# Near attention in the feed-forward: probabilities normalised on GpSimd before they are turned, results kept as [d, rows]

## The reference, cut to what matters

```python
logits = einsum('bcqgrd,bckgd->bcgrqk', qc, kb) * (d ** -0.5)   # 8 heads of 64, 2 key heads
logits = where(valid, logits + bias, NEG)
p = softmax(concatenate([logits, sink], axis=-1), axis=-1)[..., :-1]
o = einsum('bcgrqk,bckgd->bcqgrd', p, vb)
```

## Time and profile before

| | us |
|---|---|
| median of 3 runs | 3340.32 |
| lowest, highest | 3338.69, 3345.28 |
| span of the profiled execution | 3341.9 |

### The profile page before, as it was taken

The page is one execution under the profiler, slowest core; times in us unless marked ns, Lnnn a source line. Parts: engine busy times, 40 slices in busy tenths (PEclk is TensorE's granted clock), DMA queues, the critical chain, the costliest instruction groups (busy, mean ns, idle before and its releaser), DMA issues.

```text
span 3341.9 us, 43563 instructions
## 1 busy us (share of the span) xinstructions
PE 3248.2 (97%) x16120; PEld 2720.3 (81%) x16120; DVE 1947.1 (58%) x3598; ACT 1450.4 (43%) x2610; POOL 1704.8 (51%) x1077
## 2 busy tenths in 40 slices
PE   8999999999999999999999999999999999999998
PEld 6788878878777888888788887877888789878887
DVE  3236747558566556567666766867768678621112
ACT  3324435335454444345455534736655367420001
POOL 5555554454345555553555554145556731356665
PEclk9999999999999999999999999999999999999999
DMA  5745454444524333323433332063333410333332
GB/s 159 206 136 167 120 169 133 130 126 150 178 97 140 98 107 97 119 84 121 155 103 106 95 117 92 1 224 97 95 102 107 142 44 1 124 123 95 96 106 95
DMA packets 446562, 388.99 MB, mean 116 GB/s; under 512 B 20976, under 2 KB 376560, under 8 KB 445712
## 3 DMA queue, kind: packets, MB, share of 16 engines
q1 hardware_dynamic: 424912, 341.99, 33.7%
q10 hardware_dynamic: 21440, 44.22, 3.6%
HBM read 323.37 MB, written 62.78 MB: 116 GB/s over the span
## 4 chain that ended last, share of the span: by engine, by line
PE 90%; DVE 3%; ACT 3%; POOL 2%; issue 1%; DMA 1%; ACTq 0%; SPq 0%; DVEq 0%; POOLq 0%
PE BANK L849 21%; PE BANK L851 21%; PE BANK L850 21%; PE LP L849 3%; PE LP L851 3%; PE LP L850 3%; PE BANK L1072 3%; PE LP L1056 2%; PE BANK L1087 2%; PE LP L957 2%; PE LP L956 2%; PE LP L1057 2%; PE BANK L1089 1%; PE BANK L1098 1%; POOL WLO L819 1%
## 5 line engine op out<-in xcount | busy, mean ns | idle before, releaser
L817 POOL TENSOR_SCALAR WHI<-WRAW 128x1024 fp32r<-128x1024 f32 x456 | 507.6, 1113 | 1217.2 <-PE BANK L851 985.4
L819 POOL TENSOR_TENSOR WLO<-WRAW,WHI 128x1024 fp32r<-128x1024 f32 x456 | 1108.0, 2430 | 37.9
L849 PE MATMUL BANK<-H2hi,WHI 128*128 128x512 f32 x1408 | 558.3, 396 | 2.7 <-POOL WLO L819 1.9
L851 PE MATMUL BANK<-H2hi,WLO 128*128 128x512 f32 x1408 | 550.8, 391 | 0.0
L850 PE MATMUL BANK<-H2lo,WHI 128*128 128x512 f32 x1408 | 550.8, 391 | 0.0
L849 PE MATMUL BANK<-HThi,WHI 128*128 128x512 f32 (+1 forms) x1024 | 404.2, 395 | 3.4 <-DVE QS L1706 3.4
L851 PE MATMUL BANK<-HThi,WLO 128*128 128x512 f32 (+1 forms) x1024 | 399.7, 390 | 0.0
L850 PE MATMUL BANK<-HTlo,WHI 128*128 128x512 f32 (+1 forms) x1024 | 399.7, 390 | 0.0
L1443 ACT ACTIVATE MASK<-SCD,THR 128x896 bf16<-128x896 f32 (+5 forms) x186 | 281.8, 1516 | 218.5 <-DVE THR L1766 190.7
L851 PEld LDWEIGHTS BANK<-H2hi,WLO 128*128 128x128 f32 x1408 | 265.5, 189 | 56.8
L849 PEld LDWEIGHTS BANK<-H2hi,WHI 128*128 128x128 f32 x1408 | 266.1, 189 | 54.1 <-issue 2.3
(11 more groups left out here) (291 smaller groups left out, 6514.5 us busy)
## 6 DMA issues: line engine op xcount, KB each, us to landing
WRAW<-in_w_in SPq DMA_DIRECT2D x124, 512.0 KB, 4.5
WRAW<-in_w_ffn_gate SPq DMA_DIRECT2D x88, 512.0 KB, 3.9
WRAW<-in_w_ffn_up SPq DMA_DIRECT2D x88, 512.0 KB, 3.8
WRAW<-in_w_ffn_down SPq DMA_DIRECT2D x88, 512.0 KB, 3.5
qsp<-QS SPq DMA_DIRECT2D x32, 512.0 KB, 5.7
gates<-GS ACTq DMA_DIRECT2D x64, 256.0 KB, 2.2
WRAW<-in_w_out SPq DMA_DIRECT2D x32, 512.0 KB, 4.3
GL<-gates ACTq DMA_DIRECT2D x48, 256.0 KB, 4.1
```

Source lines behind the costliest of these rows:

```text
L817: nc.gpsimd.tensor_scalar(hi, raw, 1.0, 1.0, ALU.mult, ALU.mult).then_inc(w_hi, 1)
L819: nc.gpsimd.tensor_tensor(lo, raw, hi.bitcast(f32), ALU.subtract).then_inc(w_split, 1)
L849: nc.tensor.matmul(dst, whi, mhi, start=first, stop=False)
L851: return nc.tensor.matmul(dst, wlo, mhi, start=False, stop=last)
```

## The change

The sum and its inverse move forward, to two slots ahead of the first turn. GpSimd then multiplies the unit's 128 x 1024 exponentials by the inverse of their row, in place (`near_norm`), in its program behind the split of the job in which the first turn stands; PE's turns wait for that multiply. The turn-back, the scaling and the last transposes are gone. After the second value block ScalarE copies the low half (64 partitions) to `NLV`, and VectorE adds it to the high half out of the bank, with two instructions that write `OTA`. In units with `NEAR_FIRST[q] % 4` other than 1, both turns and the first value block come one slot later; the second value block and the copy come at 13 instead of 12 in all units, the adds at 14. The values bank is free for the next unit when `near_kept` is signalled by VectorE's adds, no longer by ScalarE's copy. ScalarE waits for `near_kept` ahead of the first split of `OTA`.

```diff
         def near_after(q):
-            return (2, 5, 9, 8) if NEAR_FIRST[q] % 4 == 1 else (3, 6, 10, 9)
+            return (2, 5, 9, 8) if NEAR_FIRST[q] % 4 == 1 else (3, 7, 11, 10)
+
+        NEAR_LAST = 13
...
+            def near_norm(b, q):
+                j, hs = q // 2, slice(4 * (q % 2), 4 * (q % 2) + 4)
+                pool.wait_ge(near_inverted, n(near_inverted, (b, q)))
+                nc.gpsimd.tensor_tensor(NLG[q % 2][:, :, :], NLG[q % 2][:, :, :], RS[:, j, hs].unsqueeze(2).to_broadcast([P, 4, BAND]),
+                                        ALU.mult).then_inc(near_normed, made(near_normed, (b, q)))
...
                 if key[0] != "br" or key[2] > 1:
                     split(i)
+                k, place = pair_place(key[1], key)
+                for q in NEAR[k] if k is not None else ():
+                    if place == (NEAR_FIRST[q] + near_after(q)[1]) // 2:
+                        near_norm(key[1] + 1, q)
...
-                            pe.wait_ge(near_probs, n(near_probs, (b, q)))
+                            pe.wait_ge(near_normed, n(near_normed, (b, q)))
...
-                                near.bank = take("near_values", near_copied, (b, q), ("near v", b, q))
+                                near.bank = take("near_values", near_kept, (b, q), ("near v", b, q))
...
-                    if since == 15:
-                        dst = take("near_back", near_scaled, (b, q), ("near x", b, q))
-                        pe.wait_ge(near_copied, n(near_copied, (b, q)))
-                        pe.wait_ge(fold_set, 1)
-                        for i in range(4):
-                            last = nc.tensor.matmul(dst[:, i * HD:(i + 1) * HD], NXV[:, i, :], FOLD[:, :], start=True, stop=True,
-                                                    skip_group_check=True)
-                        last.then_inc(near_back, made(near_back, (b, q)))
-                    if since == 18:
-                        dst = take("near_back", near_kept, (b, q), ("near o", b, q))
-                        for e in range(2):
-                            last = nc.tensor.transpose(dst[:, e * P:(e + 1) * P],
-                                                       NON[:, 2 * e:2 * e + 2, :].rearrange("p h d -> p (h d)"), IDENT[:, :])
-                        last.then_inc(near_out, made(near_out, (b, q)))
...
             def split_head(b, s, e):
+                if b and (s, e) == (0, 0):
+                    act.wait_ge(near_kept, n(near_kept, (b, PAIRS // 2 - 1)))
...
-                    if since == 18:
-                        act.wait_ge(near_out, n(near_out, (b, q)))
-                        nc.scalar.copy(OTA[:, 2 * g:2 * g + 2, j * P:(j + 1) * P],
-                                       in_tiles(bank(("near o", b, q)))[:, 0:2, :]).then_inc(near_kept, made(near_kept, (b, q)))
...
-                    if h - NEAR_FIRST[q] == 12:
+                    if h - NEAR_FIRST[q] == NEAR_LAST:
                         act.wait_ge(near_valued, n(near_valued, (b, 2 * q + 1)))
                         if q:
-                            act.wait_ge(near_out, n(near_out, (b, q - 1)))
-                        nc.scalar.copy(NXV[:, :, :], in_tiles(bank(("near v", b, q)))).then_inc(near_copied, made(near_copied, (b, q)))
+                            act.wait_ge(near_kept, n(near_kept, (b, q - 1)))
+                        nc.scalar.copy(NLV[0:HD, :, :], in_tiles(bank(("near v", b, q)))[HD:P, :, :]
+                                       ).then_inc(near_copied, made(near_copied, (b, q)))
...
-                    if since == 10:
+                    if since == near_after(q)[1] - 2:
                         dve.wait_ge(near_probs, n(near_probs, (b, q)))
                         nc.vector.tensor_tensor(RS[:, j, hs], RS[:, j, hs], ES[:, j, hs], ALU.add
                                                 ).then_inc(near_summed, made(near_summed, (b, q)))
...
-                    if since == 15:
-                        dve.wait_ge(near_back, n(near_back, (b, q)))
-                        dve.wait_ge(near_inverted, n(near_inverted, (b, q)))
-                        x = bank(("near x", b, q))[:, 0:4 * HD].rearrange("p (h d) -> p h d", h=4)
-                        nc.vector.tensor_tensor(NON[:, :, :], x, RS[:, j, hs].unsqueeze(2).to_broadcast([P, 4, HD]), ALU.mult
-                                                ).then_inc(near_scaled, made(near_scaled, (b, q)))
+                    if since == NEAR_LAST + 1:
+                        dve.wait_ge(near_copied, n(near_copied, (b, q)))
+                        x = bank(("near v", b, q))[0:HD, :].rearrange("d (e s r) -> d e s r", e=2, s=2)
+                        low = NLV[0:HD, :, :].rearrange("d (e s) r -> d e s r", s=2)
+                        for s in range(2):
+                            last = nc.vector.tensor_tensor(OTA[s * HD:(s + 1) * HD, 2 * g:2 * g + 2, j * P:(j + 1) * P],
+                                                           x[:, :, s, :], low[:, :, s, :], ALU.add)
+                        last.then_inc(near_kept, made(near_kept, (b, q)))
```

More of the change, by code:

```diff
@@ L187, in trunk_program @@
         NV = [at(f"NV{i}", [P, 2, P], f32r, r1 + 12288 + 1024 * i) for i in range(2)]
-        NXV, NON = at("NXV", [P, 4, P], f32, r1 + 14336), at("NON", [P, 4, HD], f32, r1 + 14336)
+        NLV = at("NLV", [P, 4, P], f32, r1 + 14336)
         NPhi = [at(f"NPhi{i}", [P, 4, P], f32r, rT + 8192 + 4096 * i) for i in range(2)]
@@ L248, in trunk_program @@
         near_copied, near_summed, near_inverted = sem("near_copied"), sem("near_summed"), sem("near_inverted")
-        near_back, near_scaled, near_out, near_kept = (sem(s) for s in ("near_back", "near_scaled", "near_out", "near_kept"))
+        near_normed, near_kept = sem("near_normed"), sem("near_kept")
         tabb_in, vb_in, comb_ready = sem("tabb_in"), sem("vb_in"), sem("comb_ready")
@@ L830, in _ @@
                          low=[(4,), (5,), (6,), (7,)], logits=[(4, 5), (6, 7)], near_scores=[(4, 5)], near_turn=[(6,)],
-                         near_values=[(7,)], near_back=[(3,)])
+                         near_values=[(7,)])
             taken, owner = {kind: 0 for kind in rings}, {}
@@ L1151, in near @@
                     _, turn, value, turn_next = near_after(q)
-                    for p, turn_after, value_after in ((2 * q, turn, value), (2 * q + 1, turn_next, 12)):
+                    for p, turn_after, value_after in ((2 * q, turn, value), (2 * q + 1, turn_next, NEAR_LAST)):
                         if since == turn_after:
                             dst = in_tiles(take("near_turn", near_ready, (b, p), ("near t", b, p)))
-                            pe.wait_ge(near_probs, n(near_probs, (b, q)))
+                            pe.wait_ge(near_normed, n(near_normed, (b, q)))
                             for t in range(2):
@@ L1335, in exps @@
                         if b and p == 0:
-                            act.wait_ge(near_scaled, n(near_scaled, (b, PAIRS // 2 - 1)))
+                            act.wait_ge(near_kept, n(near_kept, (b, PAIRS // 2 - 1)))
                         for s in range(len(chunks_of(heads[0][1]))):
```

## The result

| | us |
|---|---|
| before, median of 4 runs (lowest, highest) | 3341.65 (3338.69, 3345.28) |
| after, median of 4 runs (lowest, highest) | 3367.56 (3365.49, 3369.52) |
| ratio after to before, 95% interval | 1.0076 [1.0064, 1.0088] |
| span of the profiled execution after | 3367.0 |

I forecast 3327 us in a range of 3315 to 3338. The change makes the kernel 26 us slower: the direction was wrong. All of it lies in the three feed-forwards with near attention. From the first to the last start of the matmuls on `H2` they took 361.5, 361.3 and 366.0 us before, and 361.5, 371.5 and 381.5 after: nothing, 10.2 and 15.5 us more.

A forecast was written before the change was run, and what follows sets the result against it. PE was taken to bound the kernel, going from matmul to matmul (busy 3248.2 of 3341.9 us). Removed work and two waits, -24.2 + 5.0 + 6.1 = -13.1 us, gave a forecast of 3327 us, range 3315 to 3338.

The forecast's parts named there:

- Removed from PE: On PE, 192 turn-back matmul passes and two transposes per unit go, over 24 units: 25.2 us less, 24.2 counted.
- Multiply: On GpSimd, 24 added multiplies of 128x1024, priced at 2.40 us each, with 1.05 and 3.38 as bounds.
- First wait: PE's turn waits for the multiply on normalised probabilities: unit 0, and units 2 and 4 of blocks 2 and 3; 5.0 us.
- Second wait: PE waits for the single values bank, freed by VectorE's adds, in blocks 2 and 3, none in block 1: 6.1 us.
- The sum: Whole kernel: -24.2 + 5.0 + 6.1 = -13.1 us, span 3328.8, median 3327.2; forecast 3327, chance 0.55.
- More stalls: Rival 2's title: PE's two waits feed each other; 3338 us, range 3333 to 3342, chance 0.16.
- Off PE and DMAs at nothing: ScalarE, VectorE and DMA changes hide under weight matmuls or behind waits already there, costing nothing; no cost through the weights.
- Rival 2: PE's waits for the multiply and the values bank feed each other: 3338 us, range 3333 to 3342, chance 0.16.
- Rival 3: Dear GpSimd multiply: 13 us per us above 2.40, decides from 3.4 us; at 4.8 us near 3370; chance 0.09.
- Rival 1: VectorE's short operations reach the ports ahead of the multiply, or the values bank is in time: 3317 to 3322, chance 0.2.
- a sign of its being wrong: Multiply far from 2.4 us, PE waiting in block 1 too, or PE waiting for weights in more places.
- the signs for it: PE busy 13 to 20 us less, multiply about 2.4 us, PE waits on multiply and adds, threshold update 2.4 us late.

The follow-up runs named there:

- The square: Four runs: second turn at 9 without multiply 3319.4 us, with it 3335.6; second turn at 10 without multiply 3333.5, with it (the changed kernel) 3367.6.
- e2: e1 with VectorE's adds that free the values bank one slot earlier (13) in units with NEAR_FIRST % 4 == 3: 3326.87 us, 0.996 to before.
- e1: The changed kernel with the second turn of units with NEAR_FIRST % 4 == 3 back at slot 9 instead of 10: 3335.55 us, 0.998 to before.
- e10: e2 with the threshold update ahead of the sum and inverse on VectorE, where an inverse falls due before a search step: 3319.33 us, 0.9936 to before.

## Why the prediction was wrong

**The step that failed** is the sentence "Scores, turns and values stay in number and only move by a slot." Each move changes what stands ahead of it in the queues. For the first turn of unit 3 I did follow that its NPhi now stands behind the table load and SiLU; for the second turn, moved from 9 to 10, I followed nothing, and did not ask who takes the bank `near_turn` next. I had asked just this of `near_values`. The kernel before shows what I would have found: behind unit 1 the second count ends at 2350.50 + 2.07 = 2352.57, 0.1 us ahead of the place of unit 2's turn (2352.68), and with the turn moved, NPhi and NPlo still follow that count. These waits are 34.8 of the 38.8 us of near waits in after.

**Each cause makes the other dearer.** I had the multiply's hold on the threshold update right in kind (L1764 at 1.8 us), and priced what it does to units 2 and 4. Behind the same update stand the counts, and behind them the NPhi and NPlo that a bank hangs on. The square shows some 18 us that belong to neither cause alone.

**What the waits do afterwards was not in the sum.** PE ran its near instructions in 89.3 us before, waits included, and in 106.4 after (summed as for e2). That is 17.1 of the 25.7 us. Another 7.8 are weight matmuls at a lower clock: 48 of them start about 0.43 us apart, against 9 before, where 0.23 is the rule. My sum had no term for them. The last section shows one such stretch. The rest, 0.8, I leave open.

Point by point, with e1, which has no bank collision, for what the collision hides in after:

- **Removed from PE, 25.2 us:** right. e10, where near work hardly waits, spends 63.2 us on it; 89.3 - 63.2 = 26.1.
- **Multiply, 2.40:** it is 1.90. The nearest row was a subtraction of two full tiles; the bound was kept and holds.
- **First wait, 5.0 us:** unit 0 nothing, as near as makes no difference. Units 4 and 2 of block 3 and unit 4 of block 2 have 2.72, 2.86 and 2.72 us between starts, of which 0.12 are there without a stall (I had 1.7, 1.6 and 0.8), unit 2 of block 2 (0.7) does not stall. So the first wait is 7.9 us, 2.9 above my sum: the places were right but for one, the sizes too small, although the multiply was shorter than I took it.
- **Second wait, 6.1 us:** 1.46, 2.9 and 1.66 us between starts in block 3, 0.69 and 0.46 in block 2, of each of which 0.23 are there without a stall: 6.0 us, right by place and size.
- **The sum:** without the collision my terms give 3327 and e1 has 3335.55, inside *More stalls* (3333 to 3342). Against before on its own chip (3342.22) e1 wins 6.7 us where I had 13.1. Of the 6.4 missing, 2.9 are the first wait and 2.2 weight matmuls at the lower clock behind the stalls (20 of them start 0.43 us apart in e1, against 9 before); the rest I leave open.
- **Off PE and DMAs at nothing:** the wait for weights is 4.1 us in 4 cases, against 4.1 in 3; with those that the view lists for a matmul into `LP`, five places in both kernels: right.
- **Rival 2** had waits that feed each other. The square shows that, but for the multiply and the bank of the turns, not for the pair that it named.
- **Rival 3** put the slow side near 3370 and the time came out at 3367.6, but by another mechanism, so that is luck: the multiply was cheaper than its point of decision, not dearer.
- **Rival 1** I set aside since a split gets in at the first gap. In after it does. e10 shows that the order can be chosen. (Its sum gives 3318 to 3323, not the 3317 to 3322 written there; nothing rests on it.)

What the prediction named as a sign of its being wrong came: PE waits in block 1 too, 6.6 us in three places. And of the signs for it, the waits on the multiply were not in the list of after at all, since PE came later still for the bank; they came out in e1.

The rule that I quoted there from the Trainium skill (SBUF — State Buffer, Who interferes with whom), that the order of issue decides who blocks, is borne out by both orders: 1.79 us for the update in e2, 0.16 in e10. The same section names the form that also writes its accumulator as one that doesn't take the pair; the count in e10, of that form, agrees (1.92 us beside the multiply).

## What to carry to other kernels

When a step moves by one slot, list every buffer that it fills and every queue that it crosses, and price each buffer with one copy by its next taker: a move that looks free lost 14 us alone and 32 with the multiply beside it. Where two engines exclude each other, put the short operations that others wait for ahead of the one that releases the long operation: that order alone was worth 30 us on after. Costs that stand in one chain should be tried together, since here they came to 18 us more than their sum.

## What the runs showed of the hardware

A wait of PE can cost more than its length. Granted clock around the wait of 7.12 us (columns: stretch, us, busy us of PE, PEld, DVE, ACT, POOL, then PEclk, DMA share, GB/s), and starts of weight matmuls behind it:

```profile
2355.00:2367.70 12.70, 5.63 (x29) 4.55 (x27) 10.55 (x17) 7.93 (x16) 6.84 (x4) 0.92 0.18 52
2367.70:2373.00 5.30, 5.26 (x16) 4.32 (x17) 0.69 (x1) 1.75 (x3) 0.00 (x0) 0.55 0.26 77
2373.00:2380.00 7.00, 7.00 (x36) 5.87 (x35) 4.50 (x7) 2.35 (x3) 3.46 (x2) 1.00 0.03 7
```

```profile
2369.51 0.63 PE L864 MATMUL BANK<-H2hi,WLO 128*128 128x512 f32 x1
2369.94 0.63 PE L862 MATMUL BANK<-H2hi,WHI 128*128 128x512 f32 x1
...
2374.81 0.39 PE L863 MATMUL BANK<-H2lo,WHI 128*128 128x512 f32 x1
2375.03 0.39 PE L864 MATMUL BANK<-H2hi,WLO 128*128 128x512 f32 x1
```

Behind the wait the granted clock is 0.55 for about 5 us, so mostly at the lower level (1.2 of 2.4 GHz), and the matmuls start 0.43 us apart instead of 0.23. In after five to ten of them run so behind six of the nine waits for NPlo, 1 to 2 us lost each time: those of 7.12, 6.98, 6.11, 3.78, 2.77 and 1.90 us. Behind those of 2.92, 2.30 and 0.95 us none does, and the granted clock is 1.00 for the 5 us behind each. So the length of the wait alone does not decide it. The turn behind the wait of 7.12 us takes 1.12 us instead of 0.60.

On GpSimd the multiply whose second input is repeated along the row takes 1.90 us for 128x1024 and 1.04 for 128x512, the subtraction of two full tiles of 128x1024 2.40. The two differ in the operation and the type of the result as well, so that the repeated input is what makes it cheaper is not shown.
